# A hybrid decoder block with a mixture of experts: the last pass of the expert loop written out, and the last tile's rows added by TensorE

## The chip, the cores and the metric

The kernel runs on one core of a Trainium2 chip. The metric is the device time of one execution in microseconds (us), the median of several. Engines are TensorE (PE; PEld is its weight load), VectorE (DVE), ScalarE (ACT), GpSimd (POOL) and SyncE (SP), which issues most DMAs. The core has 16 DMA engines.

## The reference, cut to what matters

One layer on x of 512 tokens by 1024 channels: `h = x + mixer(rms_norm(x))`, then `h = h + moe(rms_norm(h))`, then a final rms norm with gain. The change touches only the expert part and the final norm:

```python
top_vals, top_idx = lax.top_k(logits, 4)            # of 32 experts, for each of 512 tokens
top_w = softmax(top_vals)
gu = xb @ w_gate_up[e] + b_gate_up[e]               # xb: the tokens of expert e; 1024 -> 2048
gate = minimum(gu[:, :1024], 7.0)
up = clip(gu[:, 1024:], -7.0, 7.0)
hid = (up + 1.0) * gate * sigmoid(1.702 * gate)
y = hid @ w_down[e] + b_down[e]                     # 1024 -> 1024
out[token] += y * top_w
result = rms_norm(h + out, norm_final_g)
```

## The kernel before

Every product in full precision is made from halves: a float32 operand is split into a high part (rounded to the type fp32r that TensorE takes in one go, by ScalarE) and a low part (what is left, by VectorE), and three products (high x high, high x low, low x high) are added in the PSUM bank.

**Items and chunks.** The expert part works in items: item i is up to 128 tokens of expert i. With these inputs there are 32 items, 0 to 31, so `last` is 31. An item's weights come in 12 chunks of 1 MB: 8 for gate and up, and 4 for down. Each chunk is loaded by SP into one of 6 buffers `mraw`, split by ScalarE (`weights_hi`, L517) into one of 4 `mhi` and by VectorE (`weights_lo`, L521) into one of 4 `mlo`, and used by TensorE (L2335 to L2338 for gate and up, L2356 to L2359 for down). `e_h`, `e_l` and `e_used` count chunks split and used; number m of 0 to 13 in the code names the chunk, with 12 and 13 those that are split ahead for the next item.

**The loop.** Each engine has a loop `Fori(0, last)`, 31 passes. In pass i TensorE waits for the two clamps of item i, makes gate and up of item i+1 (`gate_up`, banks 0 to 3) with the transposes of item i's hidden rows after its third chunk (`turn_hidden`, L2319, into `turn_bank`, banks 6 and 7), then item i's down product (`down`, into `y_bank`, banks 4 and 5) with the transposes of item i+2's tokens after the first chunk (`turn_tokens`, L2313). VectorE splits chunks and, after chunk 10, clamps the gate and up banks of item i+1 (L1827, L1829), splits one chunk, makes `(up+1)*gate` (`gated`, L1834), the low part of item i+2's tokens (L1779) and two more chunks. GpSimd multiplies by the sigmoid (`hidden`, L889), gathers item i+3's tokens (`gather`), and scatters item i's rows with addition into the token sums in DRAM (`scatter`: two one-column copies L892 and L894, a one-column operation `step` L877, the indirect DMA L899, and the load of the slot weights L907). ScalarE copies item i's rows out of the bank, times their slot weight (`y_copy`, L1287), which `scatter` waits for, as the next down product does.

**Behind the loop.** TensorE transposes the mixing weights (L2391, into bank 3; their low part is made by VectorE at L1849, ahead of the loop), then item 31's hidden rows, makes the products of the down bias with the mixing weights for token tiles 0 and 1 (`bias_product`, L2397), item 31's down product, the bias product of tile 2, and then adds item 31's rows to each token tile by a product with a matrix of zeros and ones (`put_back`; `last_rows`, L2403 and L2406). So a tile's banks hold all that item 31 and the bias give. The sums of the other items come back from DRAM into `h_rows` (called zT in the profile, whose place it shares; likewise `hid`, `gate` and `up` are glu), as soon as item 30's scatter has landed: SP waits for `s_stored`, loads the final gain and then the four tiles (L732). For each tile VectorE adds the banks to the rows (`add_products`, L1872), ScalarE squares and sums (L1334), GpSimd adds epsilon and raises to -1/2 (L951, L953), VectorE scales (`finish`, L1878) and SP stores (L736). Tile 3 is scaled and stored in two halves.

GpSimd's last pass also gathers an item 33 and TensorE transposes an item 32, which are never used.

## Time and profile before

| what | us |
|---|---|
| median of 3 runs (lowest to highest) | 1825.93 (1825.74 to 1826.26) |
| the profiled execution, its own time | 1826.16 |
| its span in the profile | 1824.2 |
| TensorE busy (share of the span) | 1793.4 (98%) |
| VectorE busy | 1452.8 (80%) |
| ScalarE busy | 1101.8 (60%) |
| GpSimd busy | 710.9 (39%) |

The splits of the expert weights are the largest groups of VectorE (L521: 384 of 2.39 us) and of ScalarE (L517: 384 of 1.91 us). The shares are means over stages with different limits: the gated delta rule and projections up to about 640 us, the routing up to 690, the expert loop from 690 to 1791, and the end. A matmul's record is longer than its turn: the next one starts before its modelled end, so steps on TensorE are taken from start to start.

### The profile page before, as it was taken

Reading aid. Unit: us, or ns where it says so; the run is one execution under the profiler, and the core shown is the slowest. Engines: PE = TensorE matmul, PEld = TensorE weight load, DVE = VectorE, ACT = ScalarE, POOL = GpSimd, SP = SyncE. Lnnn points to the kernel's source line nnn. Section 1 sums busy time; section 2 is a strip of 40 time slices with the busy share of each in tenths; the row PEclk is TensorE's granted clock in tenths of the full one; section 3 lists DMA queues with packets and bytes.
Section 4 is the critical chain, followed back from the end, with each engine's and each line's share of the span. In section 5 each row is a group of like instructions: output and inputs, shape, how many; then the busy total and the mean of one; then the engine's idle time right before and its main releaser. Section 6 shows DMA issues by size and latency. Waiting matters only on the chain. (4 is left out here: it accounts for less than half of the span.)

```text
span 1824.2 us, 24016 instructions
## 1 busy us (share of the span) xinstructions
PE 1793.4 (98%) x8620; PEld 1497.8 (82%) x8620; DVE 1452.8 (80%) x1087; ACT 1101.8 (60%) x902; POOL 710.9 (39%) x395
## 2 busy tenths in 40 slices
PE   8999999999999999999999999999999999999996
PEld 6888888897888887888888888888888888888885
DVE  4336667674334689999999999999999999999997
ACT  4223563343332356777777777777777777777774
POOL 1000112420000015654664565466456546645654
PEclk9999999999999999999999999999999999999998
DMA  5223424005442648999999999999999999999995
GB/s 186 94 93 113 165 75 134 18 11 181 150 128 92 234 182 333 368 372 391 379 373 375 383 374 369 387 376 374 376 385 372 372 388 373 376 376 380 374 368 197
DMA packets 127053, 503.87 MB, mean 276 GB/s; under 512 B 25336, under 2 KB 25544, under 8 KB 93924
## 3 DMA queue, kind: packets, MB, share of 16 engines
q1 hardware_dynamic: 114400, 478.57, 68.4%
q0 software_dynamic: 10272, 24.40, 5.8%
q10 hardware_dynamic: 2340, 0.33, 0.1%
q8 instruction: 29, 0.48, 0.1%
q14 instruction: 12, 0.10, 0.0%
HBM read 486.18 MB, written 26.26 MB: 281 GB/s over the span
## 5 line engine op out<-in xcount | busy, mean ns | idle before, releaser
L521 DVE TENSOR_TENSOR mlo<-mraw,mhi 128x2048 fp32r<-128x2048 f32 x384 | 904.7, 2393 | 52.0 <-ACT mhi L517 52.0
L517 ACT ACTIVATE mhi<-mraw 128x2048 fp32r<-128x2048 f32 x384 | 718.5, 1912 | 109.9 <-PE PB L2338 109.9
L2335 PE MATMUL PB<-mhi,xgT_hi 128*128 128x512 f32 x1024 | 403.0, 394 | 1.3 <-DVE mlo L521 1.3
L2336 PE MATMUL PB<-mlo,xgT_hi 128*128 128x512 f32 x1024 | 400.0, 391 | 0.0
L2338 PE MATMUL PB<-mhi,xgT_lo 128*128 128x512 f32 x1024 | 273.9, 389 | 0.0
L889 POOL TENSOR_TENSOR glu<-glu 128x1024 f32<-128x1024 f32 x32 | 78.9, 2466 | 459.9 <-DVE glu L1834 459.9
L2335 PEld LDWEIGHTS PB<-mhi,xgT_hi 128*128 128x128 f32 x1024 | 192.7, 188 | 42.3 <-DVE mlo L521 1.4
L2336 PEld LDWEIGHTS PB<-mlo,xgT_hi 128*128 128x128 f32 x1024 | 192.9, 188 | 39.5
L2338 PEld LDWEIGHTS PB<-mhi,xgT_lo 128*128 128x128 f32 x1024 | 192.3, 188 | 40.3
L2356 PE MATMUL PB<-mhi,hT_hi 128*128 128x512 f32 x512 | 202.1, 395 | 1.1 <-DVE hT_lo L1839 1.1
L2357 PE MATMUL PB<-mlo,hT_hi 128*128 128x512 f32 x512 | 199.4, 389 | 0.0
L2359 PE MATMUL PB<-mhi,hT_lo 128*128 128x512 f32 x512 | 158.0, 390 | 0.0
L1369 DVE TENSOR_TENSOR lo<-raw,hi 128x2048 fp32r<-128x2048 f32 x24 | 55.0, 2291 | 113.0 <-ACT hi L986 113.0
L877 POOL TENSOR_TENSOR idle<-idle 128x1 f32<-128x1 f32 x65 | 131.3, 2020 | 10.1 <-DMA token_sums_scratch<-y_rows,now 3.3
L1939 PE MATMUL PB<-xT_hi,hi 128*128 128x512 f32 x336 | 131.2, 390 | 0.7 <-ACT ab L1007 0.7
L1687 DVE TENSOR_TENSOR lo<-qkvT,hi 128x2048 fp32r<-128x2048 f32 x18 | 41.3, 2292 | 113.2 <-ACT hi L1198 113.2
L1941 PE MATMUL PB<-xT_hi,lo 128*128 128x512 f32 x336 | 130.7, 389 | 0.0
L1940 PE MATMUL PB<-xT_lo,hi 128*128 128x512 f32 x336 | 130.7, 389 | 0.0
L986 ACT ACTIVATE hi<-raw 128x2048 fp32r<-128x2048 f32 x25 | 47.8, 1914 | 124.8 <-PE PB L1941 105.0
L2356 PEld LDWEIGHTS PB<-mhi,hT_hi 128*128 128x128 f32 x512 | 96.2, 188 | 20.3 <-issue 1.5
L2359 PEld LDWEIGHTS PB<-mhi,hT_lo 128*128 128x128 f32 x512 | 96.1, 188 | 20.1
L2357 PEld LDWEIGHTS PB<-mlo,hT_hi 128*128 128x128 f32 x512 | 96.3, 188 | 18.9
(357 smaller groups left out, 2748.1 us busy)
## 6 DMA issues: line engine op xcount, KB each, us to landing
mraw<-in_w_gate_up_dram SPq DMA_DIRECT2D x256, 1024.0 KB, 9.3
mraw<-in_w_down_dram SPq DMA_DIRECT2D x128, 1024.0 KB, 7.8
raw<-in_w_in_dram SPq DMA_DIRECT2D x27, 1024.0 KB, 5.1
qkvT<-in_w_in_dram SPq DMA_DIRECT2D x8, 1024.0 KB, 5.3
qkvT<-in_w_o_gdn_dram SPq DMA_DIRECT2D x4, 1024.0 KB, 5.1
qkvT<-in_w_o_sconv_dram SPq DMA_DIRECT2D x4, 1024.0 KB, 5.0
qkvT<-in_w_mix_out_dram SPq DMA_DIRECT2D x4, 1024.0 KB, 5.1
qkvT<-in_x_dram SPq DMA_DIRECT2D x4, 512.0 KB, 5.1
```

What stands on the lines that cost most here:

```text
L517: nc.scalar.activation(mhi[split_slot(m)][:], mraw[:, raw_slot(m), :], ACT.Copy).then_inc(e_h, 1)
L521: nc.vector.tensor_tensor(mlo[split_slot(m)][:], mraw[:, raw_slot(m), :], mhi[split_slot(m)][:].bitcast(F32), ALU.subtract).then_inc(e_l, 1)
L877: nc.gpsimd.tensor_tensor(idle[:, n:n + 1], idle[:, 1:2], idle[:, 1:2], ALU.add).then_inc(s_idle, 1)
L1939: pe.matmul(dst, w_hi, xT_hi[:, k, :], start=(k == 0), stop=False)
L1940: pe.matmul(dst, w_hi, xT_lo[:, k, :], start=False, stop=False)
L1941: mm = pe.matmul(dst, w_lo, xT_hi[:, k, :], start=False, stop=(k == KD - 1))
L2335: pe.matmul(gate_up_bank[:, n, :], xgT_hi[:, k, :], w_hi[:, n, :], start=False, stop=False)
L2336: pe.matmul(gate_up_bank[:, n, :], xgT_hi[:, k, :], w_lo[:, n, :], start=False, stop=False)
L2338: mm = pe.matmul(gate_up_bank[:, n, :], xgT_lo[:, k, :], w_hi[:, n, :], start=False, stop=(k == KD - 1))
L2356: pe.matmul(y_bank[:, n, :], hT_hi[:, k, :], w_hi[:, kk, n, :], start=(k == 0), stop=False)
L2357: pe.matmul(y_bank[:, n, :], hT_hi[:, k, :], w_lo[:, kk, n, :], start=False, stop=False)
L2359: mm = pe.matmul(y_bank[:, n, :], hT_lo[:, k, :], w_hi[:, kk, n, :], start=False, stop=(k == KD - 1))
```

## The change

- TensorE's, VectorE's, ScalarE's and GpSimd's loops run one pass less; the last pass (i = 30) is written out behind them. SP's loop stays.
- TensorE: the wait for the clamps stands in `gate_up`, for the gate ahead of the bias product of banks 0 and 1, for up ahead of banks 2 and 3. In the last pass, item 30's down product has between its four chunks: the transposes of the mixing weights (`turn_mixing`), the bias product of tile 0, the transposes of item 31's hidden rows. Item 31's down product goes into banks 0 and 1 (`last_bank`) from `xgT_hi` and `xgT_lo`, which hold its hidden rows, and has the bias products of tiles 1 and 2 between its chunks.
- VectorE: the low part of the mixing weights is made in the last pass instead of ahead of the loop; there both clamps and `gated` follow each other, and then three splits.
- ScalarE: in the last pass `y_copy(30)` stands behind the high part of item 31's hidden rows and one split. `last_hi` has a place of its own, so it waits no more for item 30's scatter.
- GpSimd: no gather in the last pass.
- Tile 3: its banks are now 0 and 1. Its rows are added in the bank by two products with the identity (plain float32), ScalarE squares and VectorE scales from the bank. VectorE's add of tile 3 goes.

TensorE's rows from the end of item 30's first down chunk, before: the loop's other chunks, the branch, and what stands behind it.

```order
L2313 MATMUL PB<-ident,xg 128x128 x8
...
L2359 MATMUL PB<-mhi_84,hT_lo 128x512 x2
L2380 ISA
L2380 COMPARE_AND_BRANCH
L2386 ISA
L2391 MATMUL PB<-ident,mix_114 96x128 x4
L2319 MATMUL PB<-ident,glu 128x128 x8
L2397 MATMUL PB<-b_out,mix_wT 128x512 x4
L2351 ISA
L2356 MATMUL PB<-mhi_81,hT_hi 128x512
```

The same engine and place in the changed kernel:

```order
L2381 MATMUL PB<-mhi_81,hT_lo 128x512 x2
L2423 MATMUL PB<-ident,mix_114 96x128 x4
L2373 REGISTER_ALU
L2378 MATMUL PB<-mhi_82,hT_hi 128x512
...
L2381 MATMUL PB<-mhi_82,hT_lo 128x512 x2
L2429 MATMUL PB<-b_out,mix_wT 128x512 x2
...
L2381 MATMUL PB<-mhi_83,hT_lo 128x512 x2
L2344 MATMUL PB<-ident,glu 128x128 x8
L2373 REGISTER_ALU
L2378 MATMUL PB<-mhi_84,hT_hi 128x512
```

The mixing transposes, one bias product and the hidden transposes moved from behind the fourth chunk to behind the first, second and third (`mhi_81` to `mhi_84` are the four chunks' buffers).

VectorE from the split after which it clamps to item 31's low part, before:

```order
L521 TENSOR_TENSOR mlo_87<-mraw,mhi_83 128x2048
L1824 REGISTER_ALU
L1827 TENSOR_SCALAR glu<-PB 128x1024
L1829 TENSOR_SCALAR glu<-PB 128x1024
L521 TENSOR_TENSOR mlo_88<-mraw,mhi_84 128x2048
L1833 REGISTER_ALU
L1834 SCALAR_TENSOR_TENSOR glu<-glu 128x1024
L1779 TENSOR_TENSOR xgT_lo<-PB,xgT_hi 128x1024
L520 REGISTER_ALU
L521 TENSOR_TENSOR mlo_85<-mraw,mhi_81 128x2048
```

And in the changed kernel's last pass:

```order
L521 TENSOR_TENSOR mlo_87<-mraw,mhi_83 128x2048
L1883 TENSOR_TENSOR mix_114<-mix_w,mix_114 128x4x32
L1840 REGISTER_ALU
L1843 TENSOR_SCALAR glu<-PB 128x1024
L1845 TENSOR_SCALAR glu<-PB 128x1024
L1849 REGISTER_ALU
L1850 SCALAR_TENSOR_TENSOR glu<-glu 128x1024
L521 TENSOR_TENSOR mlo_88<-mraw,mhi_84 128x2048
L520 REGISTER_ALU
L521 TENSOR_TENSOR mlo_85<-mraw,mhi_81 128x2048
L520 REGISTER_ALU
L521 TENSOR_TENSOR mlo_86<-mraw,mhi_82 128x2048
```

The mixing weights' low part came in ahead of the clamps, the product of gate and up ahead of the split, and the tokens' low part is gone.

TensorE's last rows in the changed kernel, tile 3:

```order
L2429 MATMUL PB<-b_out,mix_wT 128x512 x2
L2455 MATMUL PB<-zT,ident 128x512 x2
L2435 MATMUL PB<-last_hi,put_back 128x512
L2438 MATMUL PB<-last_lo,put_back 128x512
L2435 MATMUL PB<-last_hi,put_back 128x512
L2438 MATMUL PB<-last_lo,put_back 128x512
```

The second row is new: two float32 products, which wait for tile 3's rows; the last four products now stand behind that wait.

The diff, cut to its core:

```diff
-        BANK_OF_TILE = (0, 2, 6, 4)
+        BANK_OF_TILE = (2, 4, 6, 0)
+        last_bank = PM[:, 0:2, :]
...
# GpSimd
-                    with pool.Fori(0, last) as i:
+                    with pool.Fori(0, last - 1) as i:
...
+                    pool.wait_ge(s_th, last)
+                    hidden(last)
+                    scatter(last - 1)
...
# ScalarE
+                    products_hi(last - 1)
+                    weights_hi(act, last - 1, 12)
                     act.wait_ge(s_mixT, 1)
                     nc.scalar.activation(mix_wT[:], ...
-                    hidden_hi(last)
+                    weights_hi(act, last - 1, 13)
+                    hidden_hi(last, xgT_hi)
                     weights_hi(act, last, 2)
+                    y_copy(last - 1)
                     weights_hi(act, last, 3)
...
-                    act.wait_ge(s_yfree, last + 1)
...
-                        act.wait_ge(s_sum, t + 1)
+                        if t < LAST:
+                            act.wait_ge(s_sum, t + 1)
+                        else:
+                            act.wait_ge(s_bo, 2 * TT)
...
# VectorE
+                    products_lo(last - 1)
+                    dve.wait_ge(s_mix3, 2)
+                    nc.vector.tensor_tensor(mix3[:, :, 2 * E:], mix_w[:], ...
+                    clamp(last)
+                    gated(last)
+                    for m in range(11, 14):
+                        weights_lo(dve, last - 1, m)
+                    hidden_lo(last, xgT_lo, xgT_hi)
...
-                    for t in range(TT):
+                    for t in range(LAST):
                         add_products(t)
...
# TensorE
+                            if not first and n % 2 == 0:
+                                pe.wait_ge((s_gate, s_up)[n // 2], i)
...
+                    gate_up(last, 0)
+                    down(last - 1, {0: turn_mixing, 1: lambda: bias_product(0), 2: lambda: turn_hidden(last)})
+                    last_down({1: second_bias, 2: lambda: bias_product(2)})
...
-                    bias_product(3)
-                    last_rows(3)
+                    bias_product(LAST)
+                    pe.wait_ge(s_back[LAST], 16)
+                    for n in range(2):
+                        pe.matmul(PM[:, BANK_OF_TILE[LAST] + n, :], ident[:, :], h_rows[:, LAST, n * GW:(n + 1) * GW],
+                                  start=False, stop=False)
+                    last_rows(LAST)
```

## Rows read from the trace of the kernel before

**Rows 1.** The chain that ended last (start us, us, what).

```profile
1796.06 8.05 DMA token_sums_scratch<-y_rows,now
...
1814.10 1.16 ACT glu L1334 x2
...
1819.50 0.75 DVE zT L1878
```

**Rows 2.** Stretch table, middle of the loop (stretch, us, each engine's busy time, PEclk, DMA share, GB/s).

```profile
1000.00:1300.00 300.00, 300.00 (x1391) 249.32 (x1390) 285.51 (x145) 224.43 (x145) 168.30 (x77) 1.00 0.99 378
```

**Rows 3.** Timeline of TensorE, last pass and end (start us, us, what, [idle before]).

```profile
1782.15 1.03 PE L2313 MATMUL PB<-ident,xg 128*128 128x128 f32 x8
...
1791.20 0.60 PE L2391 MATMUL PB<-ident,mix 128*96 128x128 f32 x4
1791.63 1.04 PE L2319 MATMUL PB<-ident,glu 128*128 128x128 f32 x8
1793.13 1.19 PE L2397 MATMUL PB<-b_out,mix_wT 96*128 96x512 f32 x4 [0.46 <-ACT mix_wT L1319]
1795.39 0.49 PE L2356 MATMUL PB<-mhi,hT_hi 128*128 128x512 f32 x1 [1.07 <-DVE hT_lo L1839]
...
1806.39 0.63 PE L2397 MATMUL PB<-b_out,mix_wT 96*128 96x512 f32 x2
...
1811.05 0.63 PE L2397 MATMUL PB<-b_out,mix_wT 96*128 96x512 f32 x2
```

**Rows 4.** Timeline of VectorE, last pass and end.

```profile
1778.86 2.29 DVE L521 TENSOR_TENSOR mlo<-mraw,mhi 128x2048 fp32r<-128x2048 f32 x1 [0.43 <-ACT mhi L517]
...
1782.20 1.22 DVE L1829 TENSOR_SCALAR glu<-PB 128x1024 f32<-128x1024 f32 x1
...
1810.27 5.06 DVE L1872 TENSOR_TENSOR zT<-PB,zT 128x1024 f32<-128x1024 f32 x4 [1.47 <-DMA zT<-token_sums_scratch]
```

**Rows 5.** Timeline of ScalarE: y_copy of items 29 and 30.

```profile
1756.07 1.11 ACT L1287 ACTIVATE y_rows<-PB,goal_f 128x1024 f32<-128x1024 f32 x1 [3.30 <-PE PB L2359]
...
1791.48 1.11 ACT L1287 ACTIVATE y_rows<-PB,goal_f 128x1024 f32<-128x1024 f32 x1 [3.29 <-PE PB L2359]
```

**Rows 6.** Timeline of GpSimd, last pass and behind it.

```profile
1786.84 2.41 POOL L889 TENSOR_TENSOR glu<-glu 128x1024 f32<-128x1024 f32 x1 [14.62 <-DVE glu L1834]
...
1791.52 2.13 POOL L877 TENSOR_TENSOR idle<-idle 128x1 f32<-128x1 f32 x1
...
1795.31 0.19 POOL L877 TENSOR_TENSOR idle<-idle 128x1 f32<-128x1 f32 x1
1796.06 3.55 POOL L899 DMA_INDIRECT token_sums_scratch<-y_rows,now  x1 [0.56 <-issue]
```

**Rows 7.** Timeline of TensorE, entry of the loop.

```profile
690.78 1.37 PE L2325 MATMUL PB<-bias,expert 128*128 128x512 f32 x4 [1.84 <-DVE glu L1829]
...
699.67 0.50 PE L2335 MATMUL PB<-mhi,xgT_hi 128*128 128x512 f32 x1 [0.62 <-DVE mlo L521]
```

**Rows 8.** Timeline of VectorE, entry of the loop.

```profile
694.91 2.51 DVE L1849 TENSOR_TENSOR mix<-mix_w,mix 128x128 fp32r<-128x128 f32 x1
```

**Rows 9.** Timeline of GpSimd, entry of the loop.

```profile
692.88 4.39 POOL L889 TENSOR_TENSOR glu<-glu 128x1024 f32<-128x1024 f32 x1 [1.76 <-DVE glu L1834]
```

**Rows 10.** Stretch table, entry of the loop and end (columns as in rows 2).

```profile
690.00:700.00 10.00, 8.60 (x29) 6.51 (x30) 10.00 (x7) 9.15 (x8) 8.24 (x5) 0.83 0.69 256
...
1815.00:1816.00 1.00, 0.00 (x0) 0.00 (x0) 0.96 (x2) 0.88 (x3) 0.58 (x2) 0.50 0.00 0
```

**Rows 11.** Timeline of TensorE: fp32 products of 256 columns.

```profile
283.88 3.61 PE L2002 MATMUL PB<-qkvT 128*128 128x256 f32 x16
```

**Rows 12.** Tile zT from 1806.1 to 1806.7: loads of tiles 2 and 3.

```profile
L732 SPq DMA_DIRECT2D zT<-token_sums_scratch x2: 432/494/556, 1805.7 to 1806.2; - x2
...
DMA to landing us min/median/max: 7.1/7.5/7.9
```

**Rows 13.** Timeline of GpSimd, final norm of tile 0, the second step.

```profile
1813.09 0.59 POOL L953 TENSOR_TENSOR fstat<-fstat,half_down 128x1 f32<-128x1 f32 x1
```

More of the change, by code:

```diff
@@ L1303, in mix_and_experts, with products_hi @@
                     last = last_item(act)
-                    with act.Fori(0, last) as i:
+                    def products_hi(i):
                         for m in range(2, 6):
@@ L1310, in mix_and_experts @@
                         sigmoid(i + 1)
+                    with act.Fori(0, last - 1) as i:
+                        products_hi(i)
                         tokens_hi(i + 2)
@@ L1847, in mix_and_experts, with products_lo @@
                     weights_lo(dve, -1, 13)
[L1848 to L1850 removed]
                     last = last_item(dve)
[L1852 removed]
+                    def products_lo(i):
                         for m in range(2, 6):
@@ L1857, in mix_and_experts @@
                             weights_lo(dve, i, m)
+                    with dve.Fori(0, last - 1) as i:
+                        products_lo(i)
                         clamp(i + 1)
@@ L2343, in gate_up, with down_chunk, down @@
                                 index_products()
-                    def down(i, m0, between=None):
+                    def down_chunk(i, m, d, bank, h_hi, h_lo):
+                        pe.wait_ge(e_l, chunk_number(i, m) + 1)
+                        w_hi, w_lo = (w[split_slot(m)][:].rearrange("p (kk n c) -> p kk n c", kk=2, n=2) for w in (mhi, mlo))
+                        for kk in range(2):
+                            k = 2 * d + kk
+                            for n in range(2):
+                                pe.matmul(bank[:, n, :], h_hi[:, k, :], w_hi[:, kk, n, :], start=(k == 0), stop=False)
+                                pe.matmul(bank[:, n, :], h_hi[:, k, :], w_lo[:, kk, n, :], start=False, stop=False)
+                            for n in range(2):
+                                mm = pe.matmul(bank[:, n, :], h_lo[:, k, :], w_hi[:, kk, n, :], start=False, stop=(k == KD - 1))
+                        mm.then_inc(e_used, 1)
+                    def down(i, after):
                         pe.wait_ge(s_hl, i + 1)
@@ L2349, in down, with last_down @@
                         for d in range(4):
-                            m = m0 + d
-                            pe.wait_ge(e_l, chunk_number(i, m) + 1)
-                            w_hi, w_lo = (w[split_slot(m)][:].rearrange("p (kk n c) -> p kk n c", kk=2, n=2) for w in (mhi, mlo))
-                            for kk in range(2):
-                                k = 2 * d + kk
-                                for n in range(2):
-                                    pe.matmul(y_bank[:, n, :], hT_hi[:, k, :], w_hi[:, kk, n, :], start=(k == 0), stop=False)
-                                    pe.matmul(y_bank[:, n, :], hT_hi[:, k, :], w_lo[:, kk, n, :], start=False, stop=False)
-                                for n in range(2):
-                                    mm = pe.matmul(y_bank[:, n, :], hT_lo[:, k, :], w_hi[:, kk, n, :], start=False, stop=(k == KD - 1))
-                            mm.then_inc(e_used, 1)
-                            if d == 0 and between is not None:
-                                turn_tokens(between)
+                            down_chunk(i, 8 + d, d, y_bank, hT_hi, hT_lo)
+                            if d in after:
+                                after[d]()
+                    def last_down(after):
+                        pe.wait_ge(s_hl, last + 1)
+                        for d in range(4):
+                            down_chunk(last, d, d, last_bank, xgT_hi, xgT_lo)
+                            if d in after:
+                                after[d]()
                     places(0)
```

61 lines of the change are left out of this document (28 added, 33 removed).

## The prediction

> **What bounds the kernel now.** I read the split of the span first, then the stretch table, then the chain that ended last, then the timelines of the two ends of the expert loop. The stretch table shows TensorE busy for all of a 300 us piece out of the middle of the expert loop, at full clock, VectorE for 95% of it and the DMA engines for 99% [rows 2]. So from the second pass to the last the loop is bound by TensorE, and the change edits nothing in a pass that repeats, except that the clamp waits stand between two matmuls instead of ahead of them; both had fired nearly 8 us earlier (1783.42 against 1791.20 in [rows 3, 4]). The middle is therefore costed at nothing; TensorE's own row of products is its cover. All that the change can move lies at the entry of the loop and in the last 45 us.
>
> The last 30 us are another matter. The chain of waits ends there in transfers: item 30's rows are scattered with addition (issued 1796.06, 8.05 us), read back, added, squared by ScalarE, passed through two GpSimd steps and scaled by VectorE, tile 3 last, from 1819.50 [rows 1]. TensorE's waits near the end (0.46 us, 1.07 us, the rows at 1793.13 and 1795.39 of [rows 3]) are not on that chain: VectorE's add of tile 0 waited for the rows to land (1810.27 in [rows 4]), not for products. So filling TensorE's waits earns nothing here. What counts is when item 30's rows are ready for the scatter, when GpSimd issues it, and what follows the landing of tile 3.
>
> **Entry of the loop.** The split of the mixing weights' low part leaves VectorE's queue there. It is recorded with 2.51 us [rows 8], and TensorE then waits 0.62 us for the next low part of the weights [rows 7]. But GpSimd's product ran 692.88 to 697.27, 4.39 us [rows 9] where the same one takes 2.41 us later [rows 6]: it waited for VectorE's split to end at 695, and VectorE's small operation then waited for it. I take it that GpSimd still gets in at 695, and that VectorE's next split waits instead. What goes is then the small operation's own time, 0.2 to 0.3 us. The other bound is the whole 2.51 us, less what TensorE can't use: it could start that chunk at about 697.9 instead of 699.67, so 1.8 us. I take -0.2.
>
> Here the trace has also this: TensorE was idle 1.84 us before 690.78 [rows 7], and from 690 to 700 its granted clock was 0.83 on average [rows 10], which is 3.4 us at 0.50, the 1.2 GHz level. In the changed kernel two bias products fall into that gap, but they only move the wait: the low part for the next chunk is still late.
>
> **Last pass, TensorE.** Before, chunk 0 (of 0 to 3) of item 30's down product ends at 1782.15 and chunk 3 at 1791.20, with the transposes of the never used item 32 between [rows 3]. A chunk is 2.75 us (1795.39 to 1806.39 are four). Now, at 1782.15, come four transposes of the mixing weights, into the bank that VectorE's second clamp reads. That clamp ends at 1783.42 [rows 4], and the small operation now stands before it, since it follows the split of 1778.86 to 1781.15: with 0.25 us for it (the 2.51 us of [rows 8] hold a wait for GpSimd, which is idle here) and 0.25 us from an end to TensorE's start, as at 690.78, TensorE goes on at 1783.9. That is a **new stall of 1.75 us**, where nothing was waited for. Then 0.43 us of transposes (1791.20 to 1791.63), chunk 1, bias product of tile 0 (half of the 1.19 us row, about 0.5), chunk 2 to 1790.3, the transposes of item 31's hidden rows (in place of those taken out) to 1791.1, chunk 3 to 1793.9. ScalarE's copy with the slot weight (y_copy) started at 1791.48, right behind chunk 3 [rows 5]; now at about 1794.15, ending 1795.25: **2.65 us later**, 1.75 of stall and 0.9 of inserted products.
>
> **Who waits for that: GpSimd.** Before, the rows were ready at 1792.6, but GpSimd was still at its small steps, the last of them at 1795.31, 0.19 us, and the scatter was issued at 1796.06 [rows 6]. So 2.7 us of the delay are covered by GpSimd's lateness, and the index steps of the never used item 33 are gone. If the same small step (it gates the scatter) could run at once at 1795.3, the scatter would go where it went: +0. But the step at 1791.52 took 2.13 us against 0.19 [rows 6]: beside VectorE's splits such a step ends when the split ends. What runs there? VectorE's order is now clamp, product, three splits, item 31's low part, two splits. The first split starts before GpSimd can begin the hidden product (as at the loop's entry), so this product ends near 1789.3, the second split is held up till then, and the third ends near 1793.7; the hidden low part follows till 1794.9, and the next split runs about 1794.9 to 1797.15. GpSimd's step, asked for at 1795.3, falls inside it and ends at 1797.2, and the scatter goes at 1797.85: +1.8. If that split came right behind ScalarE's half (1794.2), it would be +1.1. From there on VectorE has less in its way: in the 3.55 us of scatter issue [rows 6] some is waiting, and I take 0.3 us back. **Scatter and read-back: +1.5**, bounds 0 and +1.8. [...]
>
> **Last product.** Its first chunk needs item 31's low part (1794.9, so 1795.1, before 1795.39); two bias products now stand inside, so it ends near 1807.0, 0.5 us later than before. Tiles 0 to 2 are still through before their rows come back, and TensorE is through with the bias product of tile 3 by about 1812 (before, it ran from 1811.05 to 1811.5 [rows 3]).
>
> **Tile 3.** Its rows land 7.9 us after an issue near 1806.2 [rows 12], 1814.1; before, VectorE added the bank in 1.26 us (four in 5.06 [rows 4]). Now two fp32 products with the identity stand there, then four products of the last rows. The trace has no fp32 product of 512 columns. Nearest is that of 256 columns, 16 records from 283.88 to about 287.3, less the tail of the last, 0.20 each [rows 11], two records to a product; twice the columns make 0.41, and four records 1.65 us. The lower bound is the price of an ordinary 512-column product (48 in 11.00 us [rows 3]), two at 0.23; I take 1.65. The last rows add 4 x 0.23 = 0.9, and the hand-overs 0.3: 2.85 us at full clock. But TensorE has been idle for some 3.4 us by then; at the end of before, with the last products done by about 1812.6, the clock stood at 0.50 in 1815 to 1816 [rows 10]. At half clock throughout it would be 5.4 us, and since it rises again once the engine works (at the loop's entry it lasted 3.4 us), I take half of that: 4.1 us. Then ScalarE's square 1.16 [rows 1], GpSimd's two steps, 1.0 together with hand-overs (the second, longer one is 0.59 [rows 13]), since VectorE is through with tiles 0 to 2 by then. From landing to tile 3's scaling: 4.1 + 1.2 + 1.0 = 6.3 us, before 1819.50 - 1814.1 = 5.4, much of it behind VectorE's adds and scalings of other tiles. **+0.9**, with the clock up **-0.35**. The saved VectorE add is thus no gain: before, it was not what tile 3 waited for. Scaling from the bank instead of from SBUF I cost at nothing: the adds read the bank too, at 1.26 us a tile.
>
> **Sum.** Against the profiled execution's 1826.16 (its span of 1824.2 and 2.0 around it): -0.2 + 1.5 + 0.9 = +2.2, so 1828.4. That execution lies 0.2 above the median of three, so the median comes to **1828.2**, 0.12% longer: within what a measurement of this kernel can tell from no change, which I put at 0.2%, or 3.7 us (1822.3 to 1829.6).
>
> **Rivals.**
> 1. *GpSimd isn't late, the clock is up.* The small step slips in between two splits and the read-back keeps its time, tile 3 saves 0.35: -0.2 + 0 - 0.35, about 1825.4. For it: the order at that place hangs on a few tenths. Against it: every such step in the loop ends with a split.
> 2. *The entry gives more.* VectorE's split wins against GpSimd, TensorE gains 1.8 us once and keeps it, since nothing later in the loop absorbs it: -1.8 + 1.5 + 0.9, about 1826.5. Against it: [rows 8, 9].
> 3. *Slower: the new stall lowers the clock.* The place is 1782.2, after chunk 0. The idle time there (1.6 to 1.75 us) is close to the 1.84 us after which the clock went to 0.50, and well over the 1.07 us of 1795.39, after which it stayed. It decides if this wait acts as the first of these and not as the second. The 3.4 us at half clock of the loop's entry cost 1.7 us of products; chunk 3, the copy and the scatter come later by nearly all of it, as GpSimd has no lateness left to cover it: +2.2 + 1.5, about 1829.7. More goes if the small operation takes longer than 0.25 us, one for one.
> 4. *The parts don't meet as said, with a large gain:* over 3.7 us. All of the entry's 1.8, all of tile 3's add and rival 1 together make 3.6, so next to nothing.
> 5. *The written out code stalls at the loop's exit.* No engine shows idle time behind the exit of the loop before (TensorE goes on at 1791.20 [rows 3]), but that was with idle DMA engines; now the exit is at 1755. A stall would have to be over 2 us to matter.
>
> **How the numbers follow.** Forecast (between 1827 and 1829.4) 0.48; rival 1 and mixtures with it 0.20; rival 2 0.09; rival 3 0.17; rival 5 0.03; rival 4 and a larger gain 0.03. The range reaches from rival 1, 1825.2, to rival 3 with a longer small operation, 1830.4. By sign: faster by over 0.2% 0.03, slower by over 0.2% 0.17 (most of rival 3, a part of 5 and of the forecast's upper edge), same 0.80.
>
> **What would show it.** A TensorE wait of 1.5 to 2 us on the clamp ahead of the mixing weights' transposes; y_copy of item 30 some 2.65 us later against the start of its down product; GpSimd's small step ahead of the last scatter at over 1 us; the identity products at 0.8 us each at full clock or 1.6 at half, and a granted clock of 0.50 in part of that stretch; the first pass's TensorE wait still there. I am wrong if the middle of the loop changes its 35.4 us per pass (1756.07 to 1791.48 in [rows 5]), if the scatter goes no later than before, or if the identity products cost as little as ordinary ones.

## The result, and the profile after

The changed kernel takes **1828.5 us** (median of 21 runs, 1827.05 to 1829.59), the kernel before 1825.93 us (21 runs, 1825.7 to 1826.56). The ratio is 1.0012, 95% interval 1.0007 to 1.0018: 2.6 us longer, within 0.2%. The prediction said 1828.2, from 1825.2 to 1830.4. The runs lie 2.5 us apart where those of before lay 0.9 us apart; the profiled execution is the longest of them, 1829.59 us with a span of 1827.8, so what its rows show is the dear end of the range. Two of the 27 executions of the kernel before that stand beside experiments 5 to 7 (2210.89 and 3440.02 us) ran in a slow state and are left out.

Entry of the loop, TensorE's timeline (start us, us, what, [idle before]); it answers to [rows 7]:

```profile
689.32 0.72 PE L2352 MATMUL PB<-bias,expert 128*128 128x512 f32 x2 [0.52 <-DVE glu L1843]
690.45 0.74 PE L2352 MATMUL PB<-bias,expert 128*128 128x512 f32 x2 [0.41 <-DVE glu L1845]
...
699.33 0.50 PE L2362 MATMUL PB<-mhi,xgT_hi 128*128 128x512 f32 x1 [1.39 <-DVE mlo L521]
```

The idle 1.84 us is now cut into pieces of 0.4 to 0.5 us, and TensorE gets to the same chunk 0.34 us earlier. Of that 0.13 us stood already ahead of the entry (the transposes before it start at 687.77, against 687.90), so the entry gave 0.21. The stretch table, against [rows 2, 10]:

```profile
690.00:700.00 10.00, 7.48 (x30) 5.23 (x30) 10.00 (x6) 9.88 (x8) 8.24 (x4) 1.00 0.68 251
1000.00:1300.00 300.00, 300.00 (x1391) 249.50 (x1390) 285.55 (x145) 224.80 (x146) 168.64 (x77) 1.00 0.99 378
...
1815.00:1820.00 5.00, 4.74 (x7) 2.49 (x8) 3.48 (x3) 0.77 (x2) 3.22 (x3) 0.50 0.52 210
```

At the entry the granted clock stayed at 1.00 in this execution (0.83 before; the last section shows that it is not the same in every trace of either order); the middle of the loop hasn't moved, and a pass still takes 35.41 us (ScalarE's copies at 1720.31 and 1755.72); and from 1815 to 1820, where TensorE now has work on the path that sets the end, it is at 0.50, the 1.2 GHz level.

Last pass and end, TensorE's timeline, against [rows 3]:

```profile
1783.32 0.64 PE L2423 MATMUL PB<-ident,mix 128*96 128x128 f32 x4 [1.37 <-DVE glu L1845]
...
1815.26 3.78 PE L2455 MATMUL PB<-zT,ident 128*128 128x512 f32 x4 [3.31 <-DMA zT<-token_sums_scratch]
1818.05 1.42 PE L2435 MATMUL PB<-last_hi,put_back 128*128 128x512 f32 x1
```

ScalarE's copy and square, against [rows 5]:

```profile
1793.73 1.11 ACT L1294 ACTIVATE y_rows<-PB,goal_f 128x1024 f32<-128x1024 f32 x1
...
1820.78 1.02 ACT L1350 ACTIVATE glu<-PB 128x1024 f32<-128x1024 f32 x1 [5.01 <-PE PB L2438]
```

GpSimd's end, the small steps of the final norm and the scatter ahead of them, against [rows 6, 13]:

```profile
1795.01 1.72 POOL L881 TENSOR_TENSOR idle<-idle 128x1 f32<-128x1 f32 x1 [1.62 <-ACT y_rows L1294]
1796.90 3.59 POOL L903 DMA_INDIRECT token_sums_scratch<-y_rows,now  x1 [0.17 <-issue]
...
1814.87 1.46 POOL L960 TENSOR_TENSOR fstat<-fstat,half_down 128x1 f32<-128x1 f32 x1
1816.42 1.32 POOL L958 TENSOR_SCALAR fstat<-fstat 128x1 f32<-128x1 f32 x1
1817.82 0.57 POOL L960 TENSOR_TENSOR fstat<-fstat,half_down 128x1 f32<-128x1 f32 x1
1821.98 0.21 POOL L958 TENSOR_SCALAR fstat<-fstat 128x1 f32<-128x1 f32 x1 [3.60 <-ACT glu L1350]
```

VectorE's end, against [rows 4] and the last row of [rows 1]:

```profile
1810.82 3.77 DVE L1897 TENSOR_TENSOR zT<-PB,zT 128x1024 f32<-128x1024 f32 x3 [1.73 <-DMA zT<-token_sums_scratch]
1814.62 1.28 DVE L1903 SCALAR_TENSOR_TENSOR zT<-zT,fstat,final_gain 128x1024 f32<-128x1024 f32 x1
1816.37 1.28 DVE L1903 SCALAR_TENSOR_TENSOR zT<-zT,fstat,final_gain 128x1024 f32<-128x1024 f32 x1 [0.46 <-POOL fstat L960]
1818.42 1.28 DVE L1903 SCALAR_TENSOR_TENSOR zT<-zT,fstat,final_gain 128x1024 f32<-128x1024 f32 x1 [0.77 <-POOL fstat L960]
1822.87 1.41 DVE L1903 SCALAR_TENSOR_TENSOR zT<-PB,fstat,final_gain 128x512 f32<-128x512 f32 x2 [3.17 <-POOL fstat L960]
```

The chain of waits now ends through TensorE:

```profile
1796.90 8.15 DMA token_sums_scratch<-y_rows,now
1807.00 8.21 DMA zT<-token_sums_scratch
1815.26 3.78 PE PB L2455 x4
```

Read together: the scatter goes 0.84 us later (1796.06 before), tile 3's rows have landed by 1815.2 (1814.1 before), and its scaling starts 3.37 us later (1819.50 before). That is nearly the whole difference of the two profiled executions, 3.43 us. From landing to scaling it is 7.7 us where before it was 5.4. One thing in VectorE's rows was not expected: the scalings of tiles 0 to 2, 1.28 us each, start 1.75 and 2.05 us apart, each waiting for GpSimd, whose steps take 1.3 to 1.5 us instead of 0.2 to 0.6. In this execution that is not yet what tile 3 waits for: its square starts only at 1820.78, behind TensorE.

### The profile page after: what moved, and what is told of

Same layout as the page of the kernel before. It is cut to its first block, busy times and chain, and to the rows that moved or that the text cites. A ratio compares the mean times of both kernels' runs of the same rounds, so it can differ in the third digit from the quotient of the medians.

```text
span 1827.8 us, 23951 instructions
## 1 busy us (share of the span) xinstructions
PE 1796.4 (98%) x8616; PEld 1498.1 (82%) x8616; DVE 1451.8 (79%) x1085; ACT 1100.6 (60%) x900; POOL 714.7 (39%) x392
## 4 chain that ended last, share of the span: by engine, by line
PE 92%; DVE 4%; ACT 2%; DMA 1%; issue 1%; SPq 0%; POOL 0%; DVEq 0%; POOLq 0%; ACTq 0%
PE PB L2363 12%; PE PB L2362 12%; PE PB L2365 12%; PE PB L2279 11%; PE PB L2379 6%; PE PB L2381 6%; PE PB L2378 6%; PE PB L1964 4%; PE PB L1965 4%; PE PB L1966 4%; PE PB L2097 2%; PE PB L2344 2%; PE PB L2352 2%; PE PB L2338 1%; PE PB L2244 1%; DVE acc L1442 1%
## 5 line engine op out<-in xcount | busy, mean ns | idle before, releaser
L2378 PE MATMUL PB<-mhi,hT_hi 128*128 128x512 f32 x496 | 196.0, 395 | 0.0
L2379 PE MATMUL PB<-mlo,hT_hi 128*128 128x512 f32 x496 | 193.5, 390 | 0.0
L2381 PE MATMUL PB<-mhi,hT_lo 128*128 128x512 f32 x496 | 153.2, 390 | 0.0
L903 POOL DMA_INDIRECT token_sums_scratch<-y_rows,now x31 | 108.3, 3493 | 4.8 <-issue 4.8
```

The costliest lines, as they stand in the source:

```text
L2378: pe.matmul(bank[:, n, :], h_hi[:, k, :], w_hi[:, kk, n, :], start=(k == 0), stop=False)
L2379: pe.matmul(bank[:, n, :], h_hi[:, k, :], w_lo[:, kk, n, :], start=False, stop=False)
L2381: mm = pe.matmul(bank[:, n, :], h_lo[:, k, :], w_hi[:, kk, n, :], start=False, stop=(k == KD - 1))
```

## The experiments

Each kernel ran 11 times. Its median stands beside that of the kernel before on the same chip: 1826.0 us in the first four, 1826.04 in the next three, 1826.13 in the last four. The intervals of the ratios are some 0.0009 (1.6 us) to each side, wider than most steps here, so each verdict rests on the rows of the trace first and on the median second. Traces start up to 0.8 us apart in the same place of the last pass; only distances within one trace are exact. A median can't be split finer than the intervals allow: where the text below divides 2.6 us into parts, the parts are estimates.

**1. VectorE adds tile 3 again**, all else as changed.

```diff
...
-                    for t in range(LAST):
+                    for t in range(TT):
                         add_products(t)
...
-                    pe.wait_ge(s_back[LAST], 16)
-                    for n in range(2):
-                        pe.matmul(PM[:, BANK_OF_TILE[LAST] + n, :], ident[:, :], h_rows[:, LAST, n * GW:(n + 1) * GW],
-                                  start=False, stop=False)
```

The lines not shown make ScalarE's square and VectorE's scaling of tile 3 read the rows again.

> The changed kernel with tile 3 finished as before: VectorE adds the bank to the rows, ScalarE squares and VectorE scales from SBUF, no identity products. All else stays. My theory (of the 2.6 us of median loss about 1 us is the later scatter and 1.5 to 2 us the identity products behind tile 3's landing, most of it when TensorE's clock is down): about 1827.0 us, with single runs within 1 us of each other. Rival A (the loss is all in the later scatter, tile 3's route costs nothing net): 1828.5, unchanged.

Measured 1827.12 (1826.42 to 1827.60), ratio 1.0004 (0.9995 to 1.0013). VectorE's end:

```profile
1810.69 5.02 DVE L1894 TENSOR_TENSOR zT<-PB,zT 128x1024 f32<-128x1024 f32 x4 [1.72 <-DMA zT<-token_sums_scratch]
1815.75 3.68 DVE L1900 SCALAR_TENSOR_TENSOR zT<-zT,fstat,final_gain 128x1024 f32<-128x1024 f32 x3
1819.88 1.41 DVE L1900 SCALAR_TENSOR_TENSOR zT<-zT,fstat,final_gain 128x512 f32<-128x512 f32 x2 [0.46 <-POOL fstat L960]
```

So the identity products cost some 1.4 us of the 2.6, and the written-out pass some 1.1. Four of the eleven runs spend 2.5 to 2.7 us outside the span where the others and the changed kernel spend about 1.8; by the medians of the spans (1824.8, changed 1826.7, before 1824.0) the parts are 1.9 and 0.8. The order of the two is the same either way, their sizes are no better known than that. With VectorE's fourth add in place the three scalings run back to back, since GpSimd gets through its steps of the first tiles behind the adds, before a scaling stands in its way.

**2. TensorE kept busy** until tile 3's rows land, by 14 more bias products into its bank, overwritten afterwards.

```diff
+                    for r in range(14):
+                        pe.matmul(PM[:, BANK_OF_TILE[LAST] + r % 2, :], mix_wT[:, LAST, :], b_out[:, (r % 2) * GW:(r % 2 + 1) * GW],
+                                  start=True, stop=True)
                     bias_product(LAST)
```

> The changed kernel with 14 extra bias products (0.23 us each, 3.2 us) into tile 3's banks, overwritten afterwards, in TensorE's wait for tile 3's rows. They do no useful work; they only keep TensorE busy until about the landing. My theory (the spread of 2.5 us between runs and most of tile 3's price come from the granted clock, which is 0.50 there after 3.3 us of idle time): granted clock 1.00 in the identity products, each pair of records about half as long, median about 1827.1 and single runs within 1 us. Rival B (an identity product is dear at any clock, the spread has another cause): 1828.5, spread stays at 2.5 us.

Measured 1827.71 (1826.80 to 1828.52). The stretch and TensorE's rows:

```profile
1815.00:1820.00 5.00, 3.62 (x12) 1.68 (x10) 3.74 (x4) 2.41 (x6) 3.55 (x4) 1.00 0.44 178
```

```profile
1815.87 1.98 PE L2458 MATMUL PB<-zT,ident 128*128 128x512 f32 x4 [0.16 <-DMA zT<-token_sums_scratch]
1817.29 0.80 PE L2435 MATMUL PB<-last_hi,put_back 128*128 128x512 f32 x1
1817.93 0.40 PE L2438 MATMUL PB<-last_lo,put_back 128*128 128x512 f32 x1
```

At 1.00 the four records take 1.42 us from start to start, against 2.79 at 0.50 in the changed kernel: half the clock, double the time. From landing to tile 3's scaling it is 1821.10 - 1815.8 = 5.3 us instead of 7.7: in the traces the clock is worth 2.4 us. But only 0.8 us of the median came back, 0.6 less than expected, in part because most runs of the changed kernel are shorter than the profiled one. The runs lie 1.7 us apart, though their mean granted clock is 0.999 in all but one (0.998), where less than 1 us was expected: the clock isn't all of the spread. A part arises ahead of the last pass, which this trace reaches 0.58 us later than the changed kernel's (1783.90 against 1783.32). And 5.3 us is no better than before's 5.4: a second wait stands close behind the clock, though in this trace it holds tile 3 for only 0.2 us.

**3. The identity products last**, behind the four products that don't need tile 3's rows.

```diff
+                    for n in range(2):
+                        pe.matmul(PM[:, BANK_OF_TILE[LAST] + n, :], put_back[:, LAST * P:(LAST + 1) * P],
+                                  last_hi[:, n * GW:(n + 1) * GW], start=False, stop=False)
+                        pe.matmul(PM[:, BANK_OF_TILE[LAST] + n, :], put_back[:, LAST * P:(LAST + 1) * P],
+                                  last_lo[:, n * GW:(n + 1) * GW], start=False, stop=False)
                     pe.wait_ge(s_back[LAST], 16)
                     for n in range(2):
                         pe.matmul(PM[:, BANK_OF_TILE[LAST] + n, :], ident[:, :], h_rows[:, LAST, n * GW:(n + 1) * GW],
-                                  start=False, stop=False)
-                    last_rows(LAST)
+                                  start=False, stop=True).then_inc(s_bo, 1)
```

> The changed kernel with the four products of item 31's rows for tile 3 ahead of the wait for tile 3's rows, and only the two identity products behind it. My theory (what stands behind the landing is on the path, one for one): 0.9 us less at full clock, 1.7 at half, so about 1827.2. Rival A (tile 3 isn't what ends the kernel): 1828.5. The identity products then begin after the same idle time, so the spread stays at 1.5 us or more.

Measured 1827.74 (1826.94 to 1829.05), 0.5 more than expected; the spread of 2.1 us is as expected. The profiled execution (1827.10) kept its clock at 1.00. This run showed the second wait. The square of tile 3 began at 1816.55, but its scaling only at 1820.38, and GpSimd's rows say why:

```profile
1814.87 1.39 POOL L960 TENSOR_TENSOR fstat<-fstat,half_down 128x1 f32<-128x1 f32 x1
1816.35 1.32 POOL L958 TENSOR_SCALAR fstat<-fstat 128x1 f32<-128x1 f32 x1
1817.75 0.57 POOL L960 TENSOR_TENSOR fstat<-fstat,half_down 128x1 f32<-128x1 f32 x1
1818.40 1.31 POOL L958 TENSOR_SCALAR fstat<-fstat 128x1 f32<-128x1 f32 x1
1819.79 0.56 POOL L960 TENSOR_TENSOR fstat<-fstat,half_down 128x1 f32<-128x1 f32 x1
```

A step of 0.21 us is held for the length of a scaling (1.28), the next scaling waits for the step behind it, and so on: 2.05 us a tile. Taking an add off VectorE brought its scalings forward into GpSimd's steps.

**4. GpSimd's small step ahead of the copy.** The step that gates the last scatter runs before ScalarE's copy is waited for, not after.

```diff
...
-                        pool.wait_ge(s_y, i + 2)
+                        if not final:
+                            pool.wait_ge(s_y, i + 2)
                         step()
+                        if final:
+                            pool.wait_ge(s_y30, 1)
...
```

> The changed kernel, in the last pass alone: GpSimd's one-column step ahead of the scatter runs before the wait for item 30's rows instead of behind it, and the scatter waits for the rows itself. My theory (the step, 1.72 us in the trace where 0.19 is its own time, held the scatter up because VectorE's split ran beside it): scatter issued about 0.5 us after y_copy's end instead of 2.06, 1.4 us earlier, about 1827.1 us. Rival C (the scatter's own issue waits for VectorE's split as well): the issue starts earlier but lasts longer, the landing moves by less than 0.5 us, 1828.2 or more.

Measured 1826.50 (1825.65 to 1826.87), a gain of 2.0 us where 1.4 was expected. GpSimd:

```profile
1793.50 0.19 POOL L882 TENSOR_TENSOR idle<-idle 128x1 f32<-128x1 f32 x1
1795.60 2.56 POOL L907 DMA_INDIRECT token_sums_scratch<-y_rows,now  x1 [1.91 <-ACT y_rows L1298]
```

The step is 0.19 us, not 1.72, and the issue 2.56, not 3.59. The scatter costs of the written-out pass are thus the small step caught behind a split, and the issue caught behind the next one (last section; the rival that the issue waits too is right in that, but not in the landing, which moved). The gain is more than these rows alone give: tile 3's rows are in by 1812.4 instead of 1815.2, TensorE has waited 0.57 us for them instead of 3.31, and its products run at full clock (1.42 us for the four identity records). What ends this kernel is the turns of experiment 3: the scalings start at 1813.23, 1815.27, 1817.32 and 1819.35. From here on the adds wait for TensorE (1809.70, 0.66 us), no longer for the transfer.

**5. All sums stay in the banks** (on top of 3): VectorE's adds write into the banks, and squares and scalings read there. Then no scaling has two inputs in SBUF.

```diff
-            return h_rows[:, t, :] if t < LAST else last_bank.rearrange("p b c -> p (b c)")
+            return PM[:, BANK_OF_TILE[t]:BANK_OF_TILE[t] + 2, :].rearrange("p b c -> p (b c)")
...
-                        nc.vector.tensor_tensor(h, PM[:, BANK_OF_TILE[t]:BANK_OF_TILE[t] + 2, :], h, ALU.add).then_inc(s_sum, 1)
+                        nc.vector.tensor_tensor(PM[:, BANK_OF_TILE[t]:BANK_OF_TILE[t] + 2, :], PM[:, BANK_OF_TILE[t]:BANK_OF_TILE[t] + 2, :], h, ALU.add).then_inc(s_sum, 1)
```

> The kernel of the third experiment (identity products last) with one thing more: VectorE's adds of tiles 0 to 2 write into the bank instead of into the rows in SBUF, and ScalarE squares and VectorE scales all four tiles from the bank. No operation comes or goes. Theory D (new, from the traces of the third and fourth run: GpSimd's one-column steps of the final norm and VectorE's scalings exclude each other when both inputs of the scaling lie in SBUF, so they take turns at 2.05 us a tile, and this, not tile 3's landing, ends those kernels): with one input in the bank GpSimd's steps take 0.2 and 0.57 us throughout, the scalings follow at 1.2 us, tile 3's begins near 1818.5 instead of 1820.4, about 1825.9 us. Rival E (GpSimd's steps are slow beside any VectorE operation, or tile 3's path ends the kernel): 1827.7, unchanged.

Measured **1825.48** (1825.31 to 1828.11), 2.3 us less than experiment 3. The two traces, both at full clock, show 1.8 of it (tile 3's scaling at 1818.59 instead of 1820.38). The rest goes with the clock: six of experiment 3's runs have a mean granted clock of 0.996 or 0.997, one of these (the 1828.11). Why it fell less often here is open. GpSimd and VectorE:

```profile
1815.68 0.22 POOL L958 TENSOR_SCALAR fstat<-fstat 128x1 f32<-128x1 f32 x1 [0.42 <-ACT glu L1350]
1815.99 0.57 POOL L960 TENSOR_TENSOR fstat<-fstat,half_down 128x1 f32<-128x1 f32 x1
1817.70 0.21 POOL L958 TENSOR_SCALAR fstat<-fstat 128x1 f32<-128x1 f32 x1 [1.14 <-ACT glu L1350]
```

```profile
1814.48 3.67 DVE L1903 SCALAR_TENSOR_TENSOR zT<-PB,fstat,final_gain 128x1024 f32<-128x1024 f32 x3
1818.59 1.41 DVE L1903 SCALAR_TENSOR_TENSOR zT<-PB,fstat,final_gain 128x512 f32<-128x512 f32 x2 [0.43 <-POOL fstat L960]
```

GpSimd's steps run beside the scalings at their own 0.2 and 0.57 us, and the scalings of tiles 0 to 2 back to back. The turn-taking is shown to come from the scalings' second SBUF input: the adds' output and the squares' input moved as well, but the steps that changed are those beside a scaling. The Trainium skill, "SBUF — State Buffer", section on the two sides of the memory, has this rule for a VectorE operation with two SBUF inputs against a GpSimd operation that reads SBUF; these rows agree.

**6. The mixing weights' transposes one chunk later**, so that the clamp is through.

```diff
-                    down(last - 1, {0: turn_mixing, 1: lambda: bias_product(0), 2: lambda: turn_hidden(last)})
-                    last_down({1: second_bias, 2: lambda: bias_product(2)})
+                    down(last - 1, {1: turn_mixing, 2: lambda: turn_hidden(last)})
+                    last_down({0: lambda: bias_product(0), 1: second_bias, 2: lambda: bias_product(2)})
```

> The changed kernel with the mixing weights' transposes one chunk later (behind chunk 1 of item 30's down product, when the clamp has ended) and tile 0's bias product behind the first chunk of item 31's. My theory: the 1.37 us wait on the clamp goes, but TensorE then waits about 1.3 us for item 31's hidden rows, which GpSimd finishes near 1789; y_copy comes 0.9 us earlier, its rows are ready when VectorE works on the hidden low part from the bank, so GpSimd's step takes 0.2 us and the scatter goes 2 us or more earlier than 1796.9. About 1826.4 us, as the fourth experiment, since tile 0's products then come last. Rival F (the wait on the clamp is what costs, one for one): the gain is 1.4 us, 1827.1, with the scatter 1.4 us earlier.

Measured 1826.71 (1826.24 to 1827.08). TensorE's waits:

```profile
1788.95 1.09 PE L2344 MATMUL PB<-ident,glu 128*128 128x128 f32 x8 [1.15 <-POOL glu L893]
...
1794.52 0.49 PE L2378 MATMUL PB<-mhi,xgT_hi 128*128 128x512 f32 x1 [1.72 <-DVE xgT_lo L1855]
```

The clamp wait is gone, and more than its 1.37 us stands further on: 1.15 us for GpSimd's hidden product and 0.7 more for VectorE's low part. The copy still starts 0.8 us earlier (1792.92), the step misses the split and takes 0.19 us (1794.21), and that is what the gain of 1.8 us is, by the same route as in experiment 4.

**7. Experiments 4 and 1 together.**

> The changed kernel with both the first and the fourth experiment's edits: VectorE adds tile 3 as before, and GpSimd's step runs ahead of its wait. If the two losses are separate they add up: 1828.5 - 1.4 - 2.0, about 1825.1 us, 0.9 below the kernel before. If tile 0's products come last once the scatter is early (in the fourth run VectorE waited 0.66 us for them), 1825.6. If the two are one and the same loss, 1826.5.

Measured 1826.64 (1825.85 to 1827.22), the same as 4 alone, where 1825.1 to 1825.6 was expected if they were separate. VectorE's fourth add takes 1.2 us, and what it saves is the turn-taking of the first tiles; once the adds start early enough, the one pays for the other. That the gains don't add is shown; this account of it is read from the rows, not tested by itself.

**8. The identity products alone**, in the kernel before, with its last pass still in the loop.

```diff
...
-                    for t in range(TT):
+                    for t in range(LAST):
                         add_products(t)
...
                     bias_product(3)
+                    pe.wait_ge(s_back[LAST], 16)
+                    for n in range(2):
+                        pe.matmul(PM[:, BANK_OF_TILE[LAST] + n, :], ident[:, :], h_rows[:, LAST, n * GW:(n + 1) * GW],
+                                  start=False, stop=False)
                     last_rows(3)
```

> The kernel before with one half of the change: tile 3's rows are added by TensorE with the identity, squared and scaled from the bank; the last pass stays in the loop. Theory G, the halves add up: the whole change cost 2.5 us and the written-out pass with VectorE's add 0.4 to 1.1, so the identity alone costs 1.4 to 2.1; the scatter stays at 1796.1, the rows of tile 3 land near 1814.4, and finish(3) starts near 1821.5 instead of 1819.50. Time 1827.7. Rival, the identity costs only because the rows come later in the changed kernel: finish(3) near 1819.9 and 1826.3.

Measured 1826.86 (1826.12 to 1827.72), ratio 1.0004 (0.9995 to 1.0013): 0.7 us more than before, between the two theories. GpSimd and VectorE take the same turns (scalings at 1813.75, 1815.49, 1817.54), and the clock falls just as the products begin:

```profile
1813.00:1814.00 1.00, 0.25 (x1) 0.25 (x2) 0.96 (x2) 0.86 (x3) 0.55 (x3) 0.90 0.01 4
1814.00:1815.00 1.00, 1.00 (x2) 0.48 (x3) 1.00 (x1) 0.90 (x2) 1.00 (x1) 0.50 0.00 0
...
1817.00:1818.00 1.00, 1.00 (x5) 0.57 (x3) 0.46 (x1) 0.00 (x0) 0.51 (x1) 0.89 0.58 229
```

Here TensorE is back at full clock for its last three products; in the changed kernel's profiled run it wasn't for any. The two halves alone cost 0.7 and 1.1 us, together 2.6. The remaining 0.8 us is no more than the intervals leave open; how much of it is the clock of the last products is not settled.

**9. The kernel before with all its sums in the banks**: the two edits of 5, nothing else.

> The kernel before, with the sums of all four tiles written into their banks, squared and scaled from there, so that no scaling has two inputs in SBUF. Theory D (scalings with two SBUF inputs and GpSimd's steps shut each other out): GpSimd's steps of tiles 2 and 3 fall from 1.44, 0.76 and 1.46 us to 0.2 and 0.57, finish(3) starts right behind the third scaling, 1819.04 instead of 1819.50: 0.45 us less, 1825.6. Rival (the steps are long for another reason): they stay, and the time stays at 1826.0 or rises by what three more writes into banks cost.

Measured 1825.59 (1825.10 to 1826.16), ratio 0.9998 (0.9989 to 1.0007). In the kernel before, GpSimd's second steps of tiles 2 and 3 took 1.44 and 1.46 us; here, tile 3:

```profile
1816.39 0.21 POOL L954 TENSOR_SCALAR fstat<-fstat 128x1 f32<-128x1 f32 x1 [0.37 <-ACT glu L1337]
1816.69 0.56 POOL L956 TENSOR_TENSOR fstat<-fstat,half_down 128x1 f32<-128x1 f32 x1
```

All five scaling instructions run back to back (1815.19, 4.99 us), with no 0.46 us wait. So the rows confirm the rule in a kernel that nothing else was changed in. The median is 0.5 us less, as expected, but that lies within the interval and is no evidence by itself.

**10. Experiments 3, 4 and 5 in one kernel.**

> The changed kernel with three edits at once: the small GpSimd step ahead of the last scatter runs before the copy is waited for, the identity products come last, and all sums stay in the banks. If each removes a wait of its own: adds start with TensorE's products at 1809.7, three take 3.5 us, three scalings 3.7, finish(3) starts near 1817.1 instead of 1818.6 with the last two edits alone, time 1823.9. If they don't add (the stores of tile 3 bound by something else), 1825.4.

Measured **1823.96** (1823.55 to 1824.77), ratio 0.9989 (0.9980 to 0.9998): 2.2 us less than the kernel before, 4.5 less than the changed one, and the fastest here. VectorE's end:

```profile
1809.61 3.50 DVE L1901 TENSOR_TENSOR PB<-PB,zT 128x1024 f32<-128x1024 f32 x3 [0.67 <-PE PB L2442]
1813.14 4.98 DVE L1907 SCALAR_TENSOR_TENSOR zT<-PB,fstat,final_gain 128x1024 f32<-128x1024 f32 x5
```

From TensorE's products to the end VectorE never waits. Only here should the add that TensorE took over be a gain, since a fourth add (1.2 us) would now stand in an unbroken row; no kernel with it was run to show that.

**11. Kernel 10 with its waits in the last pass cleared too**: experiment 6's order, and VectorE's splits held until GpSimd's hidden product is through.

```diff
...
                     gated(last)
+                    dve.wait_ge(s_hid, last + 1)
                     for m in range(11, 14):
...
```

> The same three edits, and the mixing weights' transposes one chunk later, with VectorE's splits held until GpSimd's hidden product is through. Since the last product then takes the bias product of tile 0 inside, and nothing but TensorE holds the adds, they start 0.5 us later than in the kernel without this: 1824.4 if TensorE's order binds there. If the clamp wait that is removed (1.37 us) still reaches the end, 0.9 to 1.4 us less than that kernel, 1822.8.

Measured 1826.12 (1824.17 to 1826.67), 2.2 us *more* than kernel 10. Both theories missed it. Its runs reach from 1824.17, next to kernel 10's, to 1826.67, so the loss isn't in every run. TensorE, and its stretches:

```profile
1794.94 0.49 PE L2383 MATMUL PB<-mhi,xgT_hi 128*128 128x512 f32 x1 [2.61 <-DVE xgT_lo L1859]
...
1797.31 0.63 PE L2383 MATMUL PB<-mhi,xgT_hi 128*128 128x512 f32 x1
1797.73 0.63 PE L2384 MATMUL PB<-mlo,xgT_hi 128*128 128x512 f32 x1
```

```profile
1795.00:1797.00 2.00, 2.00 (x8) 1.63 (x9) 2.00 (x2) 0.37 (x1) 1.69 (x2) 0.85 0.49 33
1797.00:1799.00 2.00, 2.00 (x6) 1.55 (x5) 2.00 (x2) 0.00 (x0) 0.95 (x1) 0.50 0.82 137
1799.00:1801.00 2.00, 2.00 (x9) 1.61 (x8) 0.61 (x2) 0.00 (x0) 0.00 (x0) 0.80 0.49 92
```

VectorE's work in the pass is the same, so item 31's low part is ready no earlier; all but 0.65 us of TensorE's waiting now stands in one piece ahead of it, 2.61 us, and 1.4 us behind it the clock goes to 0.50 for 3.4 us (the products step by 0.43 us instead of 0.23). The adds start at 1812.13 instead of 1809.61: 0.43 from the later start, 0.5 from the bias product that now stands inside, the remaining 1.6 from the clock. The fastest run (1824.17) has a mean granted clock of 0.999, the longest two 0.997 and 0.998.

## Why the prediction held, and where it didn't

The time was right to 0.3 us in the median, with most of the mechanisms named in advance. That it was so near is partly luck: the sum was made for a profiled execution, 1828.4, and that one took 1829.59. Terms of the profiled execution, 3.43 us more than that of before:

| term | predicted | measured |
|---|---|---|
| entry | -0.2 | -0.21 |
| new clamp stall, from start to start | 1.75 | 1.52 |
| copy, less the 0.34 us ahead of it | +2.65 | +2.59 |
| scatter, less the same | +1.5 | +1.18 |
| both transfers together | 0 | +0.3 |
| landing to scaling of tile 3 | +0.9 | +2.3 |

- **Entry: right.** VectorE's next split waited for GpSimd (692.57, five in 13.31 us), so only the small operation's own time went. The prediction looked for the old wait to be still there; the bias products cut it into pieces, and TensorE waited 1.39 us instead of 0.62 for the chunk behind, so they only moved the wait, as it had said.
- **Clamp stall: right in kind, 0.2 too long.** The row's 1.37 us of idle time counts from a modelled end; from start to start, as the prediction counted, chunk 0 ends at 1781.80 and the transposes start at 1783.32. The copy came as late as predicted all the same: the inserted products cost 1.1 us where they were put at 0.9, and ScalarE's split (from 1791.81, 1.90 us) ends at the same moment. Errors cancelled.
- **The caught step: right.** It took 1.72 us, the end of the split that started at 1794.41, not at 1794.9. The prediction had this case, at +1.1, and chose the later one; +1.18 is what came. Experiment 4 removes it: 2.0 us of the median, with the slower issue and with the clock that TensorE keeps when the rows come sooner.
- **Tile 3: mis-sized, and a mechanism missing.** The four identity records were put at 1.65 us at full clock from [rows 11] and take 1.42, and the first product behind them takes 0.64 instead of 0.23; landing to square is 2.95 us (experiment 2), put at 2.85. The failing step is "I take half of that": the prediction had worked out 5.4 us for half clock throughout and chose 4.1, and in the profiled run it was 0.50 throughout, 1815.26 to 1820.78, 5.5 us. Over the 21 runs the mean granted clock goes from 0.999 in the shortest to 0.997 in the longest, so the choice of the middle fits the median better than this trace. It is also a part of the larger spread, though not all of it (experiment 2).
- **The sentence that was wrong**, in effect, is that with the clock up tile 3 would save 0.35. Experiment 2 had the clock up and from landing to scaling saved 0.1 us against before, and 3 had the square 4.2 us earlier than the profiled run and gained 0.8 in the median. GpSimd's two steps were put at 1.0 us "since VectorE is through with tiles 0 to 2 by then"; that holds only while TensorE is late (0.89 us from the first step's start to the scaling in the profiled run; in experiment 3 the scaling starts 3.83 us behind the start of the square, of which square and steps are 2.1). The prediction read in [rows 13] the step's own time, and not that the later ones were longer.
- **Rivals.** 1 (the step slips in) did not happen by itself, and experiment 4 made it happen: 1826.50 rather than 1825.4, since the turns stood in the way. 2 did not happen. 3 did not either: after 1.37 us idle the clock stayed. But its mechanism is real at 2.61 us, with a price of 1.6 us, close to the 1.7 it named (experiment 11). 5 left no sign: TensorE's products follow each other behind the loop's exit. 4 didn't happen.

## What to carry to other kernels

Before you move work off an engine, ask what its next instructions will then run beside. Here an add of 1.2 us taken off VectorE brought its scalings on top of GpSimd's 0.2 us steps, and each held the other for a whole instruction; keeping one input in the bank removed this. And work given to TensorE when it has been waiting may be paid at half clock, as here behind 2.31, 2.61 and 3.31 us: put first what needs no waiting, and count a wait that you make longer by gathering others as a risk, not only as its own length.

## What was not expected of the hardware

- **How long TensorE waited doesn't tell by itself whether its clock falls.** In the last pass and the end of these traces the granted clock stayed at 1.00 behind idle times of 1.0, 1.15, 1.37 and 1.74 us, and fell to 0.50 behind 2.31 (experiment 8), 2.61 (experiment 11) and 3.31 us. In between the same kernel does both: with 1.72 us ahead of the identity products, experiment 3's eleven runs have mean clocks of 0.999 (five, the traced one among them) and 0.996 to 0.997 (six, without a trace that shows where). At the loop's entry the same 1.84 us was followed by 0.50 in the kernel before [rows 7, 10] and in experiment 8, and by 1.00 in experiment 9 (690 to 700). And the three short waits there of 0.52, 0.41 and 0.48 us were followed by 1.00 in the changed kernel, but by 0.50 from 692.75 on in experiment 7 (0.83 on average from 690 to 700). Experiment 6 waited 2.9 us in two pieces with its clock at 1.00, experiment 11 3.3 us with one piece of 2.61; one trace of each doesn't make a rule.
- **A plain fp32 product of 512 columns** with the identity: two records, together 0.71 us at full clock and 1.40 at half, where an ordinary product's turn is 0.23. The product behind it starts 0.64 us later instead of 0.23 (experiment 2).
- **The issue of a scatter** by GpSimd lasts until 1.5 us behind the end of the VectorE split that it begins beside. In the changed kernel it began at 1796.90, the split ended at 1798.97 and the issue at 1800.49; in experiment 4 it began at 1795.60, with 1796.64 and 1798.16; in the kernel before at 1796.06, with 1798.11 and 1799.61. So it took 3.59, 2.56 and 3.55 us by how much of the split was left. In experiment 11 it began 0.34 us ahead of the split and took 1.65.
